# Opening of an encoder step rearranged: identity products on TensorE, three tiles first, and nine steps moved elsewhere

## What is computed

```python
xn = rmsnorm(x, g_attn)                                # prompt and sample rows
z  = xn @ w_in                                         # 1024 x 5640, in 128-column pieces
q, k, v, f, u, qm, gates = split(z)
o_fox  = softmax(q k^T / 8 + cumsum(log_sigmoid(f + b_f)), causal) v      # 8 heads x 64
o_pool = (trailing means of u over 2/4/8/16 rows - u) @ w_pool * s_pool   # 4 groups x 128
mk, mv = rmsnorm(mem, g_mem) @ w_mkv                   # 256 memory rows
o_mem  = softmax(qm mk^T / sqrt(128)) mv               # 4 heads x 128
h = x + (sum_b sigmoid(gate_b) * (o_b @ w_b)) @ w_out
x = h + relu(rmsnorm(h, g_mlp) @ w_up)^2 @ w_down
y = rmsnorm(x, g_final)
```

## Time and profile before

| | |
|---|---|
| three runs | 1939.59, 1940.26, 1940.54 us (median 1940.26) |
| profiled execution | 1939.99 us, span 1938.3 us, 1.7 us around it |
| TensorE matmul busy | 1900.1 us, 98% of the span |
| TensorE weight load busy | 1865.1 us, 96% |
| DVE, ACT, POOL busy | 1223.0, 843.7, 516.3 us |
| chain that ended last | PE L1600 16%, PE L1585 14%, others 1% or less |
| DMA | 202.40 MB, mean 104 GB/s |

### The profile page before, as it was taken

The page is one execution under the profiler, slowest core; times in us unless marked ns, Lnnn a source line. Parts: engine busy times, 40 slices in busy tenths (PEclk is TensorE's granted clock), DMA queues, the critical chain, the costliest instruction groups (busy, mean ns, idle before and its releaser), DMA issues. The chain is left out here.

```text
span 1938.3 us, 32954 instructions
## 1 busy us (share of the span) xinstructions
PE 1900.1 (98%) x12587; PEld 1865.1 (96%) x12587; DVE 1223.0 (63%) x2285; ACT 843.7 (44%) x1671; POOL 516.3 (27%) x547
## 2 busy tenths in 40 slices
PE   7999999999999999999999999999999999999998
PEld 7999999999999999999999999999999999999997
DVE  6675545454557665554333467687787877777765
ACT  6444435353546543442223332344444544444445
POOL 1003324150612122000000003276554333333320
PEclk9999999999999999999999999999999999999999
DMA  6451311312266633453232322233433433333323
GB/s 188 121 133 50 93 47 49 99 35 86 62 228 203 205 114 101 151 165 110 84 89 84 93 83 76 85 107 88 124 88 88 124 88 88 91 89 88 88 93 98
DMA packets 243601, 202.40 MB, mean 104 GB/s; under 512 B 16750, under 2 KB 217966, under 8 KB 243317
## 3 DMA queue, kind: packets, MB, share of 16 engines
q1 hardware_dynamic: 243445, 200.29, 34.2%
HBM read 166.62 MB, written 33.64 MB: 103 GB/s over the span
## 5 line engine op out<-in xcount | busy, mean ns | idle before, releaser
L1616 PE MATMUL ps<-act_hi,w_hi 128*128 128x384 f32 x1128 | 386.7, 343 | 1.2 <-DVE fox_q_lo L2646 0.9
L1616 PE MATMUL ps<-act_hi,w_lo 128*128 128x384 f32 x1128 | 377.9, 335 | 0.0
L1616 PE MATMUL ps<-act_lo,w_hi 128*128 128x384 f32 x1128 | 377.5, 335 | 0.0
L581 DVE TENSOR_TENSOR w_lo<-w_raw,w_hi 128x512 fp32r<-128x512 f32 (+1 forms) x200 | 197.6, 988 | 124.1 <-ACT w_hi L563 123.3
L1600 PE MATMUL ps<-ffs_hi,w_hi 128*128 128x288 f32 x832 | 245.6, 295 | 2.2 <-DVE h L2579 2.2
L1600 PE MATMUL ps<-ffs_hi,w_lo 128*128 128x288 f32 x832 | 245.3, 295 | 0.0
L1600 PE MATMUL ps<-ffs_lo,w_hi 128*128 128x288 f32 x832 | 244.9, 294 | 0.0
L1585 PE MATMUL ps<-bp_hi,pw_hi 128*128 128x288 f32 x784 | 231.5, 295 | 0.2 <-DVE pw_lo L2534 0.2
L1585 PE MATMUL ps<-bp_lo,pw_hi 128*128 128x288 f32 x784 | 231.3, 295 | 0.0
L1585 PE MATMUL ps<-bp_hi,pw_lo 128*128 128x288 f32 x784 | 231.2, 295 | 0.0
L563 ACT ACTIVATE w_hi<-w_raw 128x512 fp32r<-128x512 f32 (+1 forms) x200 | 152.7, 763 | 161.1 <-PE ps L1600 119.3
(11 more groups left out here) (352 smaller groups left out, 4181.4 us busy)
## 6 DMA issues: line engine op xcount, KB each, us to landing
w_raw<-in_w_down_dram SPq DMA_DIRECT2D x112, 256.0 KB, 3.2
pair_raw<-in_w_up_dram SPq DMA_DIRECT2D x28, 1024.0 KB, 5.4
w_raw<-in_w_in_dram SPq DMA_DIRECT2D x44, 512.0 KB, 4.2
merged<-prod SPq DMA_DIRECT2D x48, 192.0 KB, 2.0
prev<-merged SPq DMA_DIRECT2D x48, 192.0 KB, 4.1
foxs_vraw<-in_cache_fox_v_dram SPq DMA_DIRECT2D x8, 1024.0 KB, 6.1
foxs_kraw<-in_cache_fox_k_dram SPq DMA_DIRECT2D x7, 1024.0 KB, 5.4
x_in<-in_x_prompt_dram SPq DMA_DIRECT2D x8, 512.0 KB, 4.5
```

What stands on the lines that cost most here:

```text
L581: nc.vector.tensor_tensor(W[c % 2][1][:, 0:kt, :], w_raw[c % 2][:, 0:kt, :], W[c % 2][0][:, 0:kt, :].bitcast(F32), ALU.subtract).then_inc( ...
L1616: last = nc.tensor.matmul(bank(b)[:, 0:width], W[k][a][:, t, :], moving[z][:, t, j * width:(j + 1) * width], start=(t == 0 and n == 0), st ...
```

## The change

- **Opening, TensorE.** Products of the identity with itself (float32, 128 x 128, into bank 7, never read): 24 ahead of tile 0, 12 ahead of tile 1, 3 ahead of tile 2, 12 behind the turn of tile 2. Tile 2 gets banks 4 and 5 and no longer waits for DVE to leave banks 0 and 1. The halves of `EARLY` start at tile 2 and not at tile 5.
- **Opening, ACT and DVE.** `stats` and `scaled` of tiles 0, 1, 2 come first, then tiles 0 and 1 are finished, the forget weights split, tile 2 finished; then tile 3, weight piece 1, tile 4, and from tile 5 on the old loop. The banks of the early blocks are emptied at t = 6, 8, 9, 11 and not 8, 10, 11, 12; on ACT forget block 2 is emptied ahead of the split of piece 2.
- **SP.** `f_b` (8 values) is loaded right after the forget weights, not after piece 3.
- **Elsewhere** (nine moves): (1) `pool` 3 stands at the second half of q's first block; (2) ACT computes one Exp of one column at the end of `pool` 3, which brings in its table there; (3) step 24 of the sample attention over the fox cache stands one half later; (4) turning its result back is a step 25 of its own, in both sample attentions; (5) the product `br` (1,0) waits for the last sample only in its third block; (6) in three of the `mem` steps DVE makes the reciprocal ahead of the rest of the next queries (`queries_lo`); (7) at the start of each sample attention the first two `keys_lo` stand ahead of the clearing of the padded queries; (8) and (9) `down_add` of the first `down` product of rounds 0 and 5 stands ahead of the rests of that place.

```diff
@@ the table beside
-        put(("u", g + 1, 0, 0) if g + 1 < BT else ("q", 0, 0, 0), "pool", g)
+        put(("u", g + 1, 0, 0) if g + 1 < BT else ("q", 0, 0, 1), "pool", g)
...
-        put(where[3 + s], "sample", 0, s)
+        put(where[3 + s + s // (3 * NB)], "sample", 0, s)
     put(where[28], "mem_parts", 0)
+    put(where[29], "sample", 0, 3 * NB + 1)
...
+    put(where[7 + BT * QT + 5 + 3 * NB], "sample", 1, 3 * NB + 1)
@@ norm_banks
-            return ps[:, 2 * (t % 2):2 * (t % 2) + 2, :].rearrange("p a (b c) -> p (a b) c", c=P)
+            k = 4 if t == 2 else 2 * (t % 2)
+            return ps[:, k:k + 2, :].rearrange("p a (b c) -> p (a b) c", c=P)
@@ TensorE, opening
-            EARLY = {5: (0,), 6: (1,), 7: (2,), 8: (3, 4, 5), 9: (6, 7), 10: (8, 9, 10, 11)}
+            EARLY = {2: (0,), 3: (1,), 4: (2,), 5: (3,), 6: (4, 5), 7: (6,), 8: (7,), 9: (8, 9), 10: (10, 11)}
...
+            FILL = {0: 24, 1: 12, 2: 3, 3: 12}
+            def identity_products(n):
+                for _ in range(n):
+                    nc.tensor.matmul(ps[:, 7, 0:P], ident[:], ident[:], start=True, stop=True)
             for t in range(NT + MT):
+                if t < 3:
+                    identity_products(FILL[t])
                 pe.wait_ge(xn["scaled"], 2 * (t + 1))
-                if t >= 2:
+                if t >= 3:
                     pe.wait_ge(xn["done"], t - 1)
                 for k in range(KT):
                     last = nc.tensor.transpose(norm_banks(t)[:, k, :], xs[t % 3][:, k * P:(k + 1) * P], ident[:])
                 last.then_inc(xn["turned"], 1)
+                if t == 2:
+                    identity_products(FILL[3])
@@ TensorE, sample
-                    if i == NB:
-                        turned_out()
+                elif part == 1 and i == NB:
+                    turned_out()
@@ TensorE, plan
-                            if s.i == 1:
+                            if s.i == 1 and j == 2:
                                 pe.wait_ge(sa["o_done"], NB)
@@ ACT, opening (DVE: the same order of scaled, turned_lo, forget_lo, split_lo)
-            for t in range(NT + MT + 2):
+            stats(0)
+            stats(1)
+            stats(2)
+            turned_hi(0)
+            turned_hi(1)
+            forget_hi(act)
+            turned_hi(2)
+            stats(3)
+            split_hi(act, 1)
+            stats(4)
+            for t in range(5, NT + MT + 2):
...
-                if t in (8, 10, 11, 12):
-                    early(plan[(8, 10, 11, 12).index(t)])
+                if t in (6, 8, 9, 11):
+                    early(plan[(6, 8, 9, 11).index(t)])
+            early(plan[4])
             split_hi(act, 2)
-            early(plan[4])
@@ ACT, pool_hi
+                if g == BT - 1:
+                    nc.scalar.activation(small[:, 18:19], eps_t[:], ACT.Exp)
@@ DVE, mem
-                if 1 <= s <= M_UNITS:
+                if 1 <= s <= M_UNITS and not next_queries(s - 1):
                     reciprocal(u - 1)
...
-                if s % QT == 2 and s // QT + 1 < MH:
+                if next_queries(s):
+                    reciprocal(u)
                     queries_lo(s // QT + 1)
@@ DVE, items
+                early = kind == "down" and i == 0 and s in (0, SEAM // 2 - 2)
+                if early:
+                    down_add(s, i)
                 for job in prepared(n):
                     prep_lo(*job)
```

More of the change, by code:

```diff
@@ L640, in mem_pair, with next_queries @@
             return (s - 3) // 2 if s % 2 and 5 <= s <= M_UNITS + 1 else 0
+        def next_queries(s):
+            return s % QT == 2 and s // QT + 1 < MH
         def pooled_view(u):
@@ L735, in _ @@
                          allow_slow_non_contiguous=True).then_inc(raw_full[0], 16)
+            sp.dma_start(f_b[:], b_f.rearrange("l h -> h l"), allow_slow_non_contiguous=True).then_inc(fs["b_in"], 16)
             load_tile(4)
@@ L743, in _ @@
             load_weights(sp, 3)
-            sp.dma_start(f_b[:], b_f.rearrange("l h -> h l"), allow_slow_non_contiguous=True).then_inc(fs["b_in"], 16)
             sp.dma_start(s_col[:], s_pool.rearrange("l (g p) -> p (l g)", p=P),
@@ L1878, in sample @@
                     nc.scalar.activation(p, p, ACT.Copy, scale=col(RC, c)[rows]).then_inc(sa["p_ready"], 1)
-                elif part == 0:
+                elif part == 1 and i == NB:
                     out_low()
@@ L2188, in _ @@
             nc.vector.memset(u_t[0][:], 0.0).then_inc(po["clear"], 1)
-            for t in range(NT + MT + 2):
+            scaled(0)
+            scaled(1)
+            scaled(2)
+            turned_lo(0)
+            turned_lo(1)
+            forget_lo(dve)
+            turned_lo(2)
+            scaled(3)
+            split_lo(dve, 1)
+            scaled(4)
+            for t in range(5, NT + MT + 2):
                 if t < NT + MT:
                     scaled(t)
-                if t >= 2:
-                    turned_lo(t - 2)
-                if t == 4:
-                    forget_lo(dve)
-                if t == 5:
-                    split_lo(dve, 1)
+                turned_lo(t - 2)
             split_lo(dve, 2)
@@ L2395, in first @@
                     dve.wait_ge(at_s["pv_over"], PAIRS + M_PAIRS * k)
+                    keys_lo(a, 0, 0)
                     for n in range(2):
@@ L2404, in first @@
                     last.then_inc(sa["q_clear"], 1)
-                keys_lo(a, 0, part)
-                if part == 1:
+                else:
+                    keys_lo(a, 0, 1)
                     dve.wait_ge(sa["q_clear"], k + 1)
@@ L2467, in sample @@
                     masked_out()
-                if part == 0 and i == NB:
+                if part == 1 and i == NB:
                     out_sum()
@@ L2751, in _ @@
                 if kind == "down":
-                    down_add(s, i)
+                    if not early:
+                        down_add(s, i)
                     if s == CHUNKS - 2 and i >= KT // 2:
```

7 lines of the change are left out of this document (1 added, 6 removed).

## The result

| | before | changed |
|---|---|---|
| device time, median of 19 runs (us) | 1940.51 | 1944.35 |
| lowest and highest | 1939.59, 1941.80 | 1942.54, 1946.01 |
| profiled execution, and its span | 1939.99, 1938.3 | 1942.54, 1940.8 |
| TensorE busy in it, matmul records | 1900.1, 12587 | 1908.2, 12689 |

The changed kernel is slower: ratio 1.0019, 95% interval 1.0013 to 1.0025, so 3.8 us more where 0.9 less had been forecast, and 0.85 above the end of the range. Two gaps are to be told apart. The profiled execution is 2.6 us longer than that of before, where the sum said 0.8 shorter: 3.3 us lie in mis-sized terms. And that execution is the shortest of the 19, 1.8 us under their median; that of before lay 0.5 under its own.

What follows compares the result with a forecast made beforehand. TensorE, multiplying 98% of the span, was taken as the bound. Terms -4.0 + 7.0 - 0.7 + 2.7 - 3.7 - 0.9 - 0.4 - 0.8 = -0.8 against 1939.99: 1939.2, or 1939.4 as a median; range 1932 to 1943.5.

Steps and rivals of the forecast that it cites:

- the opening's term: Start to first memory product: early products at the higher clock, 45.4 in place of 49.70; -4.0 us, range 1.5 to 4.8.
- pushes the tiles back: Rival at the opening: identity products run longer at the lower rate, win only 1.5; 1941.9 us, chance 0.05.
- Pool 3: Start of k: piece 14's rest ahead of the running sums waits for its late landing; +7.0 us, clock charge included.
- The charge for the clock: Behind the wait at k: 10 products at the lower level, 0.147 us each; 1.5 us.
- The rival of 35 to 40 slow products: At k: TensorE stays at the lower level after the 7.4 us hole; 1944.5 us, chance 0.13.
- Last fox sample: Memory attention: two waits go, mqs_lo comes late (scores' wait +0.7), first turn moves later; net +2.7 us, range -1.9 to +3.5.
- The list of signs: What would show it; at memory attention, a wait of some 3 us at first scores and 1 at first turn.
- Reciprocals: Reciprocals ahead of queries_lo: three TensorE waits for POOL go, with refilling; -3.7 us, at least 2.5.
- Exp table: Loading the table early takes 1.28 us off ACT before the first attention step; -0.7 us.
- `keys_lo`: First keys_lo ahead of clearing the padded queries: -0.4 of the 0.6 us wait; nothing waited at the memory sample.
- memory sample: Step 25 of the memory sample, which nothing needs sooner: -0.9 us (0.8 and refilling).
- Round 0: down_add moved forward in round 0: -0.8 us of its 0.7 to 0.9.

Runs made afterwards that it cites:

- With fewer products: Changed kernel with 16, 9, 2 and 6 identity products in place of 24, 12, 3 and 12: 1944.91 us (1.0022).
- Where k waits for nothing: Changed kernel with pool 3 in two parts (sums ahead of q, rest behind block 0): 1934.38 us; the same with the opening of before: 1935.62.
- the late spread: Changed kernel with SyncE starting the 2112 KB spread of forget values behind the load of piece 14, not ahead of it: 1942.93 us (1.0014).
- `mqs` apart: Changed kernel with ScalarE waiting for the load of mqs_raw only before its own rounding of mqs: 1942.94 us (1.0010).

## Why the prediction was wrong

- **Opening: the step that failed.** "Identity products cost nothing if they fit: ... 0.21 us each", taken from a transpose of the same size. A transpose is one pass and a plain product of float32 two, so the price was half the true one, at both levels (0.22 and 0.43 measured), and they did not fit. Tile 3 was scaled 1.2 late, and the opening's term came to -1.7 where -4.0 stood. With fewer products the first memory product came 1.1 sooner, so the price accounts for 1.1 of the 1.4 by which this lead fell short of 4.0; but the time stayed at 1944.9, since a weight load at 79 us and the wait at k took the gain. A right price alone would not have saved the forecast. How long the first 24 products last also differs: in two other executions k starts 1.2 and 1.4 later for it, about as much as the median has lost besides. The mechanism (clock up from the first turn, tile turns of 1.04) was right. The rival "pushes the tiles back", with a chance of 0.05, had the effect (a gain of 1.5), though its reason was a clock that stays low for longer.
- **Opening, second step:** the sum stopped at the first memory product. DVE's weights at 50 us take 0.9 of the lead in the changed kernel, and with fewer products a load at 79 us turns a lead of 2.9 into 1.5. Where k waits for nothing, a lead of 2.5 at the first memory product is worth 1.2 in the medians.
- **Pool 3: right**, in order, place and size (7.0 and 7.0), the late landing included; the reason given for it was shown by the late spread. The charge for the clock was near too: 1.2 measured, 1.5 reckoned. The table load in the chain took 1.28 again (at 128.93), so the row held against the 2.66 of the Trainium skill (ScalarE: Activation LUTs, What ACT_TABLE_LOAD costs). The rival of 35 to 40 slow products did not come: there were 8. That its time, 1944.5, is nearly the measured one is chance.
- **Last fox sample: the size was right (2.4 for 2.7), in part by luck.** Up to the first scores it costs 0.4 (0.7 reckoned). The slow products behind the 2.3 us wait cost 1.5 and were not in the sum; the first turn, which was to add the other 2.0, waits 0.16. (The list of signs had a wait of 1 there, which does not fit the sum.) Of the 2.4 about half is the landing of `mqs_raw` with the slow products behind it (1.1 won in the trace with `mqs` apart), the rest DVE's work.
- **Reciprocals** 3.3 for 3.7, Exp table, `keys_lo` and memory sample as forecast. These sizes come from the two timelines; no run undoes one of these moves by itself.
- **Round 0: wrong by 0.8.** The wait was struck out without asking what comes next, which had been asked for round 5: the add moved ahead of `w_lo` delays the next weights.
- **The median.** The sum was set against one profiled execution and 0.2 added, but the changed kernel's median lies 1.8 above its profiled execution, 1.3 more than before's 0.5. Its runs spread over 3.5 us where before had 2.2. Nothing in the sum allowed for a cost that differs from run to run.

The forecast lay near zero because two large terms and many small ones nearly cancelled, and the range was drawn around that sum. The three largest errors of the terms (2.3, 0.8, 0.4) had one sign: each was a gain that came out smaller than forecast, and in the first two what stands behind the gain was not followed far enough.

## What to carry to other kernels

A wait struck off the list is worth its length only if the trace shows nothing within that length behind it: follow each gain to the next landing or the next weights before it is counted. Moving a job past a weight split turns round their order on every engine that serves both; the wait arises there, not on the engine the move was made for, and splitting the job at the point that the waiting engine needs wins more than either order. Price a filler by an instruction of its own kind, and measure whether it is worth anything at the end: here it was worth 0.4 us, within the scatter.

## What was not expected of the hardware

- A plain float32 product of the 128x128 identity with itself stands as two records, 0.21 us each at the lower level and 0.11 at the higher; a transpose of the same size stands as one, of 0.21 and 0.11.
- With the same instructions from 1.6 us on, the passes turned to the higher rate at 4.5 us in one execution and at 6.4 in another.
- Single waits of 2.3 to 9.0 us behind the opening were followed by 8 to 16 products at the lower level, in all traces that had one; one of 1.2 was not, nor were 1.3 and 0.8 within 3 us. Waits of 1.1, 0.4 and 0.8 within 4 us were in one trace, and 0.96, 0.40 and 0.78 at the same place in another were not.
- SyncE's issue of the load behind the 2112 KB spread took 2.4 us, and the one ahead of it, with the spread late, 0.5.
